# Subtracting the two maps of a differential head on GpSimd in two instructions instead of on VectorE in one

## What is computed

```python
h = _layer_norm(x) * (1.0 + sc_a) + sh_a
proj = h @ w_in[l]
o_na = _neighbourhood_attention(...)            # 8 heads, one map each
# differential attention, 4 heads, in blocks of 128 queries:
    logits = jnp.einsum('bqhmd,bkhmd->bhmqk', qi, k) * (d ** -0.5) + bias[None, :, None]
    p = jax.nn.softmax(logits, axis=-1)
    w = (p[:, :, 0] - lam * p[:, :, 1]).astype(v.dtype)
    o = jnp.einsum('bhqk,bkhe->bqhe', w, v)     # then a per-head RMSNorm
mix = jnp.concatenate([o_na, o_diff], axis=-1) @ w_out[l]
x = _layer_norm(DN_ALPHA * x + (1.0 + g_a) * mix, ln1_g[l], ln1_b[l])
h = _layer_norm(x) * (1.0 + sc_f) + sh_f
f = _peer(h, ...)                               # top 16 of 128*128 experts, 8 heads, per token
x = _layer_norm(DN_ALPHA * x + (1.0 + g_f) * f, ln2_g[l], ln2_b[l])
```

## Time and profile before

| | us |
|---|---|
| median of 3 runs | 1751.28 |
| lowest and highest | 1751.17, 1754.83 |
| span of the profiled execution | 1756.3 |
| TensorE busy in it | 1479.7 (84%) |
| VectorE busy | 1140.1 (65%) |
| ScalarE busy | 432.3 (25%) |
| GpSimd busy | 985.6 (56%) |

### The profile page before, as it was taken

The page is one execution under the profiler, slowest core; times in us unless marked ns, Lnnn a source line. Parts: engine busy times, 40 slices in busy tenths (PEclk is TensorE's granted clock), DMA queues, the critical chain, the costliest instruction groups (busy, mean ns, idle before and its releaser), DMA issues.

```text
span 1756.3 us, 14526 instructions
## 1 busy us (share of the span) xinstructions
PE 1479.7 (84%) x4096; PEld 684.0 (39%) x4096; DVE 1140.1 (65%) x2797; ACT 432.3 (25%) x1096; POOL 985.6 (56%) x1055
## 2 busy tenths in 40 slices
PE   5999989879899989977798799987899777777776
PEld 5444455654454345422343344432344222222222
DVE  6543055777867657776767666776666766677753
ACT  2111142441322222222222222322222222222221
POOL 1000000036767757777776677777777777777771
PEclk9899997989999999999999999999999999999999
DMA  9869221069999999999999999999999999999993
GB/s 308 326 224 218 96 72 21 7 242 374 390 388 409 406 366 391 409 409 409 409 409 408 408 409 409 410 410 409 410 409 409 409 409 409 410 409 409 410 409 152
DMA packets 190679, 606.02 MB, mean 345 GB/s; under 512 B 30704, under 2 KB 31112, under 8 KB 190440
## 3 DMA queue, kind: packets, MB, share of 16 engines
q0 software_dynamic: 147456, 536.94, 77.1%
q1 hardware_dynamic: 41799, 64.29, 11.3%
q10 hardware_dynamic: 1344, 3.87, 0.8%
HBM read 601.68 MB, written 3.34 MB: 344 GB/s over the span
## 4 chain that ended last, share of the span: by engine, by line
DMA 40%; PE 27%; POOL 14%; DVE 11%; issue 7%; ACT 1%; SPq 0%; DVEq 0%; POOLq 0%; ACTq 0%
DMA big<-in_expert_down,expert_idx 14%; DMA big<-in_expert_up,expert_idx 13%; PE pair L633 12%; POOL big L623 11%; PE pair L837 9%; DMA region_v<-in_expert_down,expert_idx 6%; DMA region_v<-in_expert_up,expert_idx 6%; POOL region_v L623 3%; PE pair L691 3%; DVE big L1379 3%; DVE big L1212 1%; DMA big<-in_w_ada 1%; PE pair L665 1%; PE pair L785 1%; DVE region_v L1379 1%
## 5 line engine op out<-in xcount | busy, mean ns | idle before, releaser
L837 PE MATMUL pair<-big 128*128 128x512 f32 x1460 | 710.1, 610 | 159.7 <-DMA big<-in_expert_up,expert_idx 147.0
L1379 DVE CUSTOM_DVE_ANT_0 big<-big,pair 128x1024 f32<-128x1024 f32 x363 | 442.6, 1220 | 250.1 <-DMA big<-in_expert_down,expert_idx 245.7
L837 PEld LDWEIGHTS pair<-big 128*128 128x128 f32 x1460 | 252.0, 190 | 547.3 <-issue 502.7
L623 POOL DMA_INDIRECT big<-in_expert_down,expert_idx x363 | 344.3, 948 | 150.1 <-issue 91.8
L623 POOL DMA_INDIRECT big<-in_expert_up,expert_idx x365 | 348.4, 955 | 127.1 <-issue 79.5
L837 PE MATMUL pair<-region_v,big 128*128 128x512 f32 x588 | 284.2, 606 | 61.6 <-DMA region_v<-in_expert_up,expert_idx 58.6
L1379 DVE CUSTOM_DVE_ANT_0 region_v<-region_v,pair 128x1024 f32<-128x1024 f32 x149 | 181.5, 1220 | 100.3 <-DMA region_v<-in_expert_down,expert_idx 97.7
L1026 ACT ACTIVATE big<-ident,big 128x128 f32<-128x128 f32 x512 | 167.1, 391 | 311.2 <-DVE big L1336 311.2
L633 PE MATMUL pair<-big 128*128 128x512 f32 (+1 forms) x480 | 194.2, 599 | 0.0
L837 PEld LDWEIGHTS pair<-region_v,big 128*128 128x128 f32 x588 | 101.8, 190 | 208.1 <-issue 187.9
L582 POOL TENSOR_SCALAR small<-small 128x4 f32<-128x4 f32 (+1 forms) x6 | 1.4, 236 | 318.6 <-DVE small L1308 282.1
(11 more groups left out here) (148 smaller groups left out, 1029.4 us busy)
## 6 DMA issues: line engine op xcount, KB each, us to landing
big<-in_w_ada SPq DMA_DIRECT2D x12, 2048.0 KB, 18.2
big<-in_w_in SPq DMA_DIRECT2D x6, 2048.0 KB, 17.0
big<-in_w_query SPq DMA_DIRECT2D x5, 2048.0 KB, 18.9
big<-in_expert_up,expert_idx POOLq DMA_INDIRECT x365, 15.5
big<-in_expert_down,expert_idx POOLq DMA_INDIRECT x363, 15.3
big<-in_w_out SPq DMA_DIRECT2D x2, 2048.0 KB, 10.3
big<-na_scr SPq DMA_DIRECT2D x24, 128.0 KB, 5.0
region_v<-in_expert_down,expert_idx POOLq DMA_INDIRECT x149, 13.0
```

The lines of the kernel that those rows point to most:

```text
L623: nc.gpsimd.indirect_dma_start(places[place], None, (expert_down if kind == "down" else expert_up)[0], bass.IndirectOffsetOnAxis(expert_id ...
L837: last = nc.tensor.matmul(pair[t % 2][:, s * HALF:(s + 1) * HALF], diag[:, j, :], places[place][:, s * HALF:(s + 1) * HALF], start=(h == 0 ...
L1379: v.tensor_tensor_reduce(out=places[place], in0=places[place], in1=u_cur[:, :], scale=1.0, scalar=0.0, op0=ALU.mult, op1=ALU.add, accum_ou ...
```

## The change

The subtraction leaves `finish_maps`. VectorE now ends with the ratio and counts up a new semaphore, `ratio_ready`. GpSimd waits for it, multiplies map 1 by the ratio in place, waits for its own instruction, adds map 1 to map 0, and counts up `diff_done`. So that the new waits can't block each other, GpSimd's list now follows `FIRST_GROUPS`, with the first five `rsqrt` at their places in it. The gathers stand behind the loop, and so behind the last subtraction.

```diff
+            def subtract_maps(a):
+
+                if maps_of(a) == 2:
+                    lo = (a % 3) * 2
+                    pool.wait_ge(ratio_ready, DIFFS_BEFORE[a + 1])
+                    link(nc.gpsimd.tensor_scalar(diff_probs[:, 1, :], diff_probs[:, 1, :], ratio[:, lo:lo + 1], None,
+                                                 ALU.mult))
+                    nc.gpsimd.tensor_tensor(diff_probs[:, 0, :], diff_probs[:, 0, :], diff_probs[:, 1, :],
+                                            ALU.add).then_inc(diff_done, 1)
...
-            for n, which in enumerate([heads, rows, rows, heads, heads]):
-                rsqrt(*which, n)
+            norms = 0
+            for kind, args in FIRST_GROUPS:
+                if kind == "values" and ATT[args[0]][1] == NA_HEADS + DIFF_HEADS - 1 and norms < 5:
+                    rsqrt(*heads, norms)
+                    norms += 1
+                if kind == "scores" and args[1] == maps_of(args[0]) - 1:
+                    if args[0] >= 1:
+                        subtract_maps(args[0] - 1)
+                    for step in LN_FIRST.get(args[0], ()):
+                        if step in (1, 5):
+                            rsqrt(*rows, norms)
+                            norms += 1
+                if kind == "probs_t" and args[0] == len(ATT) - 2:
+                    subtract_maps(len(ATT) - 1)
...
     if n == 2:
-        link(v.scalar_tensor_tensor(out=ratio[:, lo:lo + 1], in0=row_inv[:, lo + 1:lo + 2], scalar=neg_lambda,
-                                    in1=row_sum[:, lo:lo + 1], op0=ALU.mult, op1=ALU.mult))
-        v.scalar_tensor_tensor(out=diff_probs[:, 0, :], in0=diff_probs[:, 1, :], scalar=ratio[:, lo:lo + 1],
-                               in1=diff_probs[:, 0, :], op0=ALU.mult, op1=ALU.add).then_inc(diff_done, 1)
+        v.scalar_tensor_tensor(out=ratio[:, lo:lo + 1], in0=row_inv[:, lo + 1:lo + 2], scalar=neg_lambda,
+                               in1=row_sum[:, lo:lo + 1], op0=ALU.mult, op1=ALU.mult).then_inc(ratio_ready, 1)
```

More of the change, by code:

```diff
@@ L428, in build @@
         diff_done = sem("diff_done")
+        ratio_ready = sem("ratio_ready")
         mixed_ready = sem("mixed_ready")
@@ L1312, in _ @@
                 if kind == "scores" and args[1] == maps_of(args[0]) - 1 and args[0] >= 1:
-                    finish_maps(v, dve, link, dve_evac, args[0] - 1, row_inv, row_sum, exp_done, neg_lambda, ratio, diff_probs, diff_done)
+                    finish_maps(v, dve, link, dve_evac, args[0] - 1, row_inv, row_sum, exp_done, neg_lambda, ratio, ratio_ready)
                 if kind == "probs_t" and args[0] == len(ATT) - 2:
-                    finish_maps(v, dve, link, dve_evac, len(ATT) - 1, row_inv, row_sum, exp_done, neg_lambda, ratio, diff_probs, diff_done)
+                    finish_maps(v, dve, link, dve_evac, len(ATT) - 1, row_inv, row_sum, exp_done, neg_lambda, ratio, ratio_ready)
                 if kind == "out" and args[0] == 0:
@@ L1403, in _, with finish_maps @@
             finish(TILES - 1)
-def finish_maps(v, dve, link, dve_evac, a, row_inv, row_sum, exp_done, neg_lambda, ratio, diff_probs, diff_done):
+def finish_maps(v, dve, link, dve_evac, a, row_inv, row_sum, exp_done, neg_lambda, ratio, ratio_ready):
     lo = (a % 3) * 2
```

## The result

The changed kernel takes 1800.96 us (median of 4 runs, 1799.19 to 1803.61), the kernel before, run beside it, 1752.7 us (1751.17 to 1754.83). The ratio is 1.0269, with an interval from 1.0255 to 1.0283: 48 us slower. The prediction said slower, 1770 us, and at most 1785. The direction was right; the size was not, and the range didn't hold the time. The profiled execution has a span of 1800.5 us (before 1756.3).

What follows compares the result with a forecast made beforehand. TensorE, later VectorE, was taken to bound the attention, and DMA the gather stream after it. Heads 12.5 us, clock 5 and gathers 1.0 make 18.5 over a median of 1751.28: about 1770 us, range 1757 to 1785.

Steps and rivals of the forecast that it cites:

- What bounds the kernel: TensorE, in a later stretch VectorE, bounds the attention; DMA bounds the gathers after it, and the attention's delay passes on whole.
- The chain's form: From ratio start to transposes: 0.55 us plus GpSimd's multiplication and addition, where 1.16 us stood before.
- The addition, 1.25 us: GpSimd's addition of the two maps per differential head: 1.25 us, two inputs read one after the other.
- The multiplication, 0.65 us: GpSimd's multiplication of a map by the ratio: fixed 0.2 us plus 512 columns at 0.86 ns; upper end 1.14 us.
- r: Growth per differential head of the chain from ratio to transposes: 1.3 us, with ends of -0.15 and 2.8.
- The sum over 16 heads: Attention delay: nine heads that pay fully 11.4 us, three with slack 0.9, four where VectorE is late 0.2; 12.5 us.
- The clock, 5 us, at most 15: TensorE falling to half rate after holes in the attention: two to three further falls in effect, 5 us; ends 0 and 15.
- half clock nearly throughout: Rival: TensorE at half rate nearly throughout the attention, eight falls, 15 us, total 1780 us; chance 0.17.
- VectorE 12 us less busy: Sign: with the subtractions gone from the attention, VectorE's busy time falls by 12 us.
- TensorE's wait of 25 us: Sign: TensorE's wait for the transposes in the attention grows from 10.1 to about 25 us, now for GpSimd.
- The gathers: Gathers issued behind the last subtraction: 1.0 us later (0.5 to 1.8), first at about 390 us, four in a row.
- The shared port: VectorE and GpSimd excluding each other in SBUF: no blocking seen; as rival six meetings, 5 us on top, 1775; chance 0.15.

Runs made afterwards that it cites:

- e11_filler8: The changed kernel with eight idle products on TensorE ahead of each wait for GpSimd's sum; ratio 1.0183 to the kernel before, attention 23.1 us longer.
- f1_filler8: A second run of the changed kernel with eight idle TensorE products ahead of each wait for the sum; ratio 1.0174, median 31.8 us over the kernel before.

## Why the prediction was right or wrong

**What bounds the kernel.** Right. The stream from the fifth gather on is unchanged, and the attention's 47.5 us are the result's 48.

**The chain's form.** Right: 0.55 + a + b with the measured a = 1.57 and b = 1.26 gives 3.38 us, and 3.38 us is measured.

**The addition, 1.25 us.** Right, 1.26.

**The multiplication, 0.65 us.** Wrong, and this is the first step that failed, for some 10 of the missing 30 us: 1.57 us, over its upper end of 1.14 too. I took the slope of a fill, 0.86 ns per column, for an instruction that reads and writes; the measured slope is 2.5 ns. The upper end was the select of 128 columns times four, a form that this one isn't. The prediction named the sign, "lasts over 1.2 us". So r is 2.2 us, not 1.3.

By the Trainium skill (GPSIMD Engine Reference, 3.1 Elementwise — side-by-side cycle accounting) I had estimated 0.77 us for it and 1.12 for the addition; the addition agrees roughly, the multiplication with a scalar operand doesn't, by a factor of two, and only the copy (0.61 us) is that quick.

**The sum over 16 heads.** Right in its total, in part by luck: 12.5 us for r = 1.3 is 9.6 us per microsecond of chain, and with the clock nearly held it measured 9 to 11. With r = 2.2 and the slacks as they were the sum comes to 23 to 27 us, and 23.1 and 29.2 are measured. The shares of the heads did not come out. The four where VectorE is late (the 12th to 15th, by the waits of before) were put at 0.2 us; from the ratio of the first of them to the ratio of the last head it was 32.8 us before, 39.7 in e11_filler8 and 44.1 in the changed kernel, so they lose 6.9 us even with the clock held. The eleven ahead of them lose 13 us there, less than r each. Before the change some of these ran at half rate (the first one's transposes took 1.11 us), and the idle products took that away as well.

**The clock, 5 us, at most 15.** Wrong, the second failed step, and the larger one: where 5 us stood, idle products give back 18 and 24 us by the two traces and 16 by the medians. The prediction argued that a fall makes TensorE late and so fills the next hole. Here it doesn't: a TensorE at half rate still waits 2.57 us for the next sum, as the timeline shows, idles again and stays at half rate: 0.66 from 250 to 270 us. That is the rival "half clock nearly throughout", to which I gave 0.17 and 15 us, with a multiplication of 0.65 us under it. A shorter multiplication would not have saved the step: at 1.07 and 1.66 us of growth the medians grew by 16.3 and 37.4 us, and idle products gave back 5 and 19 of them.

**VectorE 12 us less busy.** Wrong: 1136.2 us against 1140.1 on the page, 4 less. The 16 subtractions are gone, but in the attention three L1145 are 1.08 us longer each, twelve L1142 have a mean of 437 ns where it was 280, two L1198 1166 where it was 692: 6.0 us. It hardly mattered, since VectorE mostly waits now.

**TensorE's wait of 25 us.** It is 47.6, at all 16 heads; 10.1 us and 16 times 2.2 would be 45.3, so no head's slack swallows it.

**The gathers.** First gather at 417.06, not 390, in a row as said. The 0.5 us for the late issue is 0.6 in the trace; the rest of the 1.0 us can't be told from zero in the changed kernel. On a chip with a slower stream the kernel with the order alone was 6.6 us slower, for a reason that stays open.

**The shared port.** I read from one meeting that nothing blocks. That holds for the form met there, 128x4 operands, which this change doesn't use. For wide operands with two inputs the rule of the Trainium skill (SBUF — State Buffer, Who interferes with whom) is what the rows show: 1.78 us beside a 1.26 us addition. As a rival it had the mechanism right. Its price, 5 us, is neither confirmed nor excluded: 0.8 us in the chain and 6.0 on a VectorE that mostly waits are what the rows show, and with the clock held nothing of it shows in the whole.

## What to carry to other kernels

Look at how long a chain between engines is, and at what TensorE does in the meantime, before you move work to an engine that is free: here 12 us taken from VectorE made 48 us more. Take the price of an instruction from a row of the same form and width, never from a fill or a narrow one, and where there is none, keep a range as wide as two forms differ. If the added wait makes TensorE idle in every period, look at the granted clock before you count on one stall hiding the next: here the clock cost between 0.4 times the delay and as much again.

## What the runs showed of the hardware

- GpSimd, 128x512 in float32: copy 0.61 us, product with a broadcast second input 1.04, addition 1.26, product with a constant 1.49, with a scalar operand from memory 1.56. The one-input forms with arithmetic take the longest.
- GpSimd and VectorE hold each other up on wide operands: with two inputs on VectorE 693 ns became 1777 beside a GpSimd addition, and GpSimd's 1.57 us became 2.07. Four one-input VectorE instructions of 128x128 went from 0.87 us to 1.66 beside a GpSimd multiplication. Beside GpSimd fills the two-input one kept its 691 ns and the four took 1.09 us.
- TensorE at a granted clock of 0.66 over 40 us in which it was busy three quarters of the time; with idle products in the holes 1.00 in the same stretch (e11_filler8), and by the medians 16 us less for the kernel (f1_filler8) though its chain is as long but for 0.1 us. The same kernel showed falls in one execution that it didn't in another (attention 173.1 and 179.2 us).
